# Expert lists in DRAM, token blocks as the stationary operand, routed rows added by DMA

## Chip, cores and metric

The kernel runs on one core of a Trainium2 chip. The metric is the time of one execution in device microseconds (us); the kernel before takes 2146.92 us, the median of three runs.

## What is computed

The reference is one step of a decoder layer for 1024 prompt tokens and 64 sample tokens, all in float32 with a model width of 1024. After a mixer stage comes the part that the change touches, a mixture of experts with 64 experts, 8 for each token, of hidden width 256:

```python
def swiglu(x, w_gate, w_up, w_down):
    return (jax.nn.silu(x @ w_gate) * (x @ w_up)) @ w_down
...
    scores = jax.nn.sigmoid(xf.astype(jnp.float32) @ w_router.astype(jnp.float32))
...
    _, idx = lax.top_k(jnp.where(emask, biased, -jnp.inf), TOP_K)
    sel = jnp.take_along_axis(scores, idx, axis=1)
    wts = (sel / jnp.sum(sel, axis=-1, keepdims=True) * ROUTED_SCALE).astype(xf.dtype)
    routed = routed_experts(xf, idx, wts, w_gate, w_up, w_down)
```

Each token's residual gets the weighted sum of its eight experts' outputs and a shared expert's. Then a per-layer embedding is added through a gate, `h + (p @ W_proj) * sigmoid(rmsnorm(h) @ W_gate)`, and a last norm gives the output.

## The kernel before

The names PE (TensorE), ACT (ScalarE), DVE (VectorE), POOL (GpSimd) and SP (SyncE) are those of the profile. Each stage is a block in which every engine runs its own instruction stream in order, and engines wait for each other by semaphores; a block ends when all engines are through. Tokens lie in 9 tiles of 128 (the last holds the 64 sample tokens).

**Router** (`router`, from L827). For each tile DVE normalises the rows (L1048), SP stores them to `rows_dram`, and PE computes the 64 scores and the shared expert. A long chain of small DVE operations picks the eight experts (`choose`), forms the weights (`weights`) and, from a running count, each token's place within its experts (`places`, L1124 to L1131). Places go to the table `place`, and the slot of every pair of token and expert to `slots`. At the end DVE works out `slots` and the number of rounds. A round handles up to CAP = 212 tokens of every expert; here there is one round.

**Experts** (`experts`, L1255 to L1566). Each expert's up to 212 tokens are two blocks, 128 and 84 rows (`BLK`). The matmuls have float32 accuracy out of reduced-precision ones: each operand x is split into hi(x), which ACT rounds, and lo(x) = x - hi(x), which DVE subtracts, and `three` (L1361) adds hi*hi, hi*lo and lo*hi. Weights are split the same way in each expert (L176, L183): 3 MB from DRAM into `raw_g`, `raw_u`, `raw_d`, one buffer each, by SP. For expert m:

- The list is made two experts ahead: DVE compares the places with 1 to 212 (`one_hot`, L1504), 18 small PE matmuls turn that into token numbers (`make_list`, L1374), DVE makes them integers (`to_index`, L1516), and POOL gathers the rows with two indirect DMAs (L1352).
- PE transposes the rows of the next expert (L1387), ACT and DVE split them (`x_hi`, `x_lo`).
- The gate and up products have the weights as the stationary operand and all 212 tokens as the moving one: 96 matmuls into two banks, transposed. After the sigmoid (L1479) DVE forms the hidden values and splits them.
- The down product has a block of tokens as the stationary operand and 512 columns of weights as the moving one: 12 matmuls for the first block, 12 for the second, which a branch on the expert's count skips (L1406 to L1412).
- ACT copies the result (L1457) and stores both blocks to `y_dram` (L1464).

The order on PE is gate and up, list, transposes of the next expert, down:

```python
                with pe.Fori(0, E) as n:
                    pe.wait_ge(x_lo_ev, 4 * (r * NJ + n) + 5)
                    gate_up(r * E + n)
                    make_list(r * NL + n + 2, r * NH + n + 2, 4 * (r * NJ + n) + 5)
                    transposes(r * NJ + n + 1, r * NL + n + 2)
                    down(r * E + n)
```

**Output** (`output`, L1573). For each tile POOL gathers the eight expert rows of each token from `y_dram` (`gathers`, L1652), and DVE adds them with their weights to the residual in SBUF (`gather_sum`, L1784). Then come the norm (L1789), the transposes (L1704), the gate matmuls (L1713), the projection (L1722), the injection and the last norm (L1812).

## Time and profile before

| | |
|---|---|
| time, median of 3 runs (lowest to highest) | 2146.92 us (2145.25 to 2151.26) |
| profiled execution, first to last instruction | 2147.0 us |
| PE busy | 1883.8 us (88%) |
| DVE busy | 1348.0 us (63%) |
| ACT busy | 868.2 us (40%) |
| POOL busy | 400.5 us (19%) |
| read from and written to DRAM | 330.71 and 66.34 MB |

The profiled execution's own time is its span: the page gives no other, and it equals the median to 0.1 us. A busy share is a mean over stages with different limits, so the stretches and timelines of the section on rows say more.
### The profile page before, as it was taken

What the parts mean: (1) busy time and instruction counts of PE and PEld (TensorE: products, weight loads), DVE (VectorE), ACT (ScalarE), POOL (GpSimd) and SP (SyncE); (2) the same over time, 40 slices, a digit from 0 to 9 for tenths busy, and PEclk for the clock granted to TensorE, in tenths of its full rate; (3) what the DMA queues carried; (4) which work ended last, traced back from release to release, by engine and by line L of the source; (5) the groups of instructions that cost most, each with busy time, mean ns of one, the idle gap of its engine ahead of it and who ended that gap; (6) DMA issues with size and microseconds to landing.
All of it is one profiled execution on the core that took longest, in us unless ns stands there. A gap on an engine that the chain in (4) does not pass through costs nothing. (4 is left out here: it accounts for less than half of the span.)

```text
span 2147.0 us, 35537 instructions
## 1 busy us (share of the span) xinstructions
PE 1883.8 (88%) x12638; PEld 1525.1 (71%) x12639; DVE 1348.0 (63%) x2002; ACT 868.2 (40%) x1392; POOL 400.5 (19%) x367
## 2 busy tenths in 40 slices
PE   7999999789968998899999989989989898747887
PEld 4566665457757897888888878888888798633433
DVE  3333433269856786767777777767666677556774
ACT  2122222133224555455555545555545555431111
POOL 0100001000011111211111121121111112135662
PEclk9999999889979998999999999999989899878999
DMA  9000000210066776767777777777676687655652
GB/s 358 35 0 0 0 0 13 85 52 29 30 208 221 255 267 219 258 225 252 263 251 246 258 244 248 251 258 264 227 254 235 226 277 247 214 203 179 229 199 103
DMA packets 104971, 396.27 MB, mean 185 GB/s; under 512 B 13230, under 2 KB 26990, under 8 KB 87901
## 3 DMA queue, kind: packets, MB, share of 16 engines
q1 hardware_dynamic: 61877, 245.27, 34.3%
q0 software_dynamic: 27264, 95.08, 13.0%
q10 hardware_dynamic: 15808, 55.65, 6.4%
q8 instruction: 12, 0.20, 0.0%
q14 instruction: 10, 0.08, 0.0%
HBM read 330.71 MB, written 66.34 MB: 185 GB/s over the span
## 5 line engine op out<-in xcount | busy, mean ns | idle before, releaser
L1352 POOL DMA_INDIRECT rows<-rows_dram,idx x132 | 228.2, 1728 | 1085.0 <-issue 1085.0
L1364 PE MATMUL GU<-x_hi,hi_g 128*128 128x212 f32 x1024 | 283.2, 277 | 0.0
L1364 PE MATMUL GU<-x_hi,hi_u 128*128 128x212 f32 x1024 | 282.7, 276 | 0.0
L1364 PE MATMUL GU<-x_lo,hi_g 128*128 128x212 f32 x1024 | 281.6, 275 | 0.0
L1364 PE MATMUL GU<-x_hi,lo_g 128*128 128x212 f32 x1024 | 281.2, 275 | 0.0
L1364 PE MATMUL GU<-x_lo,hi_u 128*128 128x212 f32 x1024 | 280.7, 274 | 0.0
L1364 PE MATMUL GU<-x_hi,lo_u 128*128 128x212 f32 x1024 | 280.3, 274 | 0.0
L1387 PE MATMUL T<-ident,rows 128*128 128x128 f32 (+1 forms) x1040 | 149.3, 314 | 137.9 <-DMA rows<-rows_dram,idx 137.9
L1522 DVE TENSOR_TENSOR x_lo<-T,x_hi 128x424 fp32r<-128x424 f32 x260 | 145.5, 595 | 144.8 <-ACT x_hi L1447 135.8
L1387 PEld LDWEIGHTS T<-ident,rows 128*128 128x128 f32 (+1 forms) x1040 | 132.9, 178 | 140.9 <-issue 140.9
L183 DVE TENSOR_TENSOR lo_u<-raw_u,hi_u 128x2048 fp32r<-128x2048 f32 x65 | 149.0, 2293 | 124.8 <-ACT hi_u L176 124.8
L1447 ACT ACTIVATE x_hi<-T 128x424 fp32r<-128x424 f32 x260 | 125.1, 527 | 220.1 <-PE T L1387 219.9
L1364 PEld LDWEIGHTS GU<-x_hi,hi_g 128*128 128x128 f32 x1024 | 197.3, 193 | 3.8
L1364 PEld LDWEIGHTS GU<-x_lo,hi_g 128*128 128x128 f32 x1024 | 197.3, 193 | 2.9
L1364 PEld LDWEIGHTS GU<-x_hi,lo_g 128*128 128x128 f32 x1024 | 197.6, 193 | 0.0
L1364 PEld LDWEIGHTS GU<-x_hi,hi_u 128*128 128x128 f32 x1024 | 196.6, 192 | 0.0
L1364 PEld LDWEIGHTS GU<-x_lo,hi_u 128*128 128x128 f32 x1024 | 196.6, 192 | 0.0
L1364 PEld LDWEIGHTS GU<-x_hi,lo_u 128*128 128x128 f32 x1024 | 196.6, 192 | 0.0
L1457 ACT ACTIVATE y<-Y 128x512 f32<-128x512 f32 (+1 forms) x256 | 150.8, 602 | 97.0 <-PE Y L1364 76.3
L183 DVE TENSOR_TENSOR lo_g<-raw_g,hi_g 128x2048 fp32r<-128x2048 f32 x65 | 148.8, 2290 | 60.5 <-ACT hi_g L176 60.5
L183 DVE TENSOR_TENSOR lo_d<-raw_d,hi_d 128x2048 fp32r<-128x2048 f32 x65 | 149.4, 2298 | 47.9 <-ACT hi_d L176 47.9
L1364 PE MATMUL Y<-hi_d,h_hi 128*128 128x512 f32 (+1 forms) x384 | 173.6, 452 | 0.0
(240 smaller groups left out, 3481.0 us busy)
## 6 DMA issues: line engine op xcount, KB each, us to landing
raw_g<-in_w_exp_gate SPq DMA_DIRECT2D x65, 1024.0 KB, 7.0
raw_u<-in_w_exp_up SPq DMA_DIRECT2D x65, 1024.0 KB
raw_d<-in_w_exp_down SPq DMA_DIRECT2D x65, 1024.0 KB, 7.7
y_dram<-y ACTq DMA_DIRECT2D x64, 512.0 KB
y_dram<-y ACTq DMA_DIRECT2D x64, 336.0 KB
rows_dram<-row SPq DMA_DIRECT2D x9, 512.0 KB, 2.7
w_big<-in_w_in SPq DMA_DIRECT2D x2, 2048.0 KB, 12.4
w_out<-in_w_out SPq DMA_DIRECT2D x1, 4096.0 KB, 18.1
```

The source lines that it names most:

```text
L183: dve.tensor_tensor(lo[:], raw[:], hi[:].bitcast(F32), ALU.subtract).then_inc(keep[f"lo_set_{name}"], 1)
L1352: pool.indirect_dma_start(out=rows[0:BLK[b], b, :], out_offset=None, in_=rows_dram[:, :], in_offset=bass.IndirectOffsetOnAxis(ap=idx[0:BLK ...
L1364: ins = pe.matmul(out, lhs[x], rhs[w], start=first and i == 0, stop=last and i == 2)
L1387: ins = pe.transpose(bank[:, k * CAP + b * P:k * CAP + b * P + BLK[b]], rows[0:BLK[b], b, (2 * i + k) * P:(2 * i + k + 1) * P], ident[0:BL ...
L1447: act.activation(x_hi[:, 2 * i:2 * i + 2, :], T[i][:, 0:2 * CAP].rearrange("p (k q) -> p k q", k=2), ACT.Copy).then_inc(x_hi_ev, 1)
L1457: act.activation(y[0:BLK[b], b, half * 512:(half + 1) * 512], Y[half][0:BLK[b], :], ACT.Copy).then_inc(y_ev, 1)
L1522: dve.tensor_tensor(x_lo[:, w, :], T[i][:, 0:2 * CAP].rearrange("p (k q) -> p k q", k=2), x_hi[:, w, :].bitcast(F32), ALU.subtract).then_i ...
```

## The change

**Router.** `place`, `slots` and the matmuls and comparisons on one-hot tables are gone. For each tile DVE works out, for each of the eight experts of a token, its position in a list in DRAM, and POOL scatters pairs (token number, weight) there with eight indirect DMAs. The list is filled beforehand, by a DMA in the mixer stage, with zero weights and spare rows (`list0`). At the stage's end SP loads the whole list as a table, and DVE copies it into `idx_t` (token numbers) and `w_t` (weights). SP also stores the residual with the shared expert's part to `acc_dram`, tile by tile.

**Experts.** The two blocks have buffers and semaphores of their own. A block of tokens is the stationary operand of the gate and up products, and 512 columns, 256 of the gate weights and 256 of the up weights, are the moving one: 24 matmuls a block, tokens on the partitions. The hidden values are then transposed (two PE transposes a block) before they are split. PE branches once for each expert: with 128 tokens or fewer the second block's matmuls and transposes are left out. ACT, DVE and POOL handle both blocks in any case. Gate and up splits have two buffers, and weights are loaded and split in halves. ACT scales the result with the weights `w_t` as it copies it, and POOL adds the rows to `acc_dram` with an indirect DMA that accumulates, one for each block; it waits until both of the expert before have landed. Gathers go out an expert ahead.

**Output.** The gathers and weighted sums are gone; SP loads the residual from `acc_dram`.

The diff, cut to its core: first the split helpers, then the router (DVE, SP, POOL, DVE), the experts (POOL, PE, ACT, DVE) and the output.

```diff
+def split_hi(act, keep, m, e, par, h):
+    act.wait_ge(keep[f"{m}_ld{h}"], 16 * e + 16)
+    act.activation(part_of(keep, "hi", m, par, h), part_of(keep, "raw", m, par, h),
+                   ACT.Copy).then_inc(keep[f"hi_set_{m}"], 1)
+def split_lo(dve, keep, m, e, par, h):
+    dve.wait_ge(keep[f"hi_set_{m}"], 2 * e + h + 1)
+    dve.tensor_tensor(part_of(keep, "lo", m, par, h), part_of(keep, "raw", m, par, h),
+                      part_of(keep, "hi", m, par, h).bitcast(F32), ALU.subtract).then_inc(keep[f"lo_set_{m}"], 1)
...
-                own.did(dve.tensor_copy(place[:, 0:E, t], pe_pos[:]))
+                own.did(dve.tensor_tensor(
+                    past[:], pos8[:].rearrange("p (k r) -> p k r", r=1).broadcast_to([P, TOP, ROUNDS - 1]),
+                    limits.rearrange("p (a r) -> p a r", a=1).broadcast_to([P, TOP, ROUNDS - 1]), ALU.is_gt))
+                own.wait()
+                own.did(dve.tensor_reduce(spot[:, 0, :], past[:], AX.X, ALU.add))
+                own.wait()
+                own.did(dve.scalar_tensor_tensor(out=spot[:, 1, :], in0=spot[:, 0, :], scalar=float(ROUND_ROWS - CAP),
+                                                 in1=pos8[:], op0=ALU.mult, op1=ALU.add))
+                own.wait()
+                own.did(dve.scalar_tensor_tensor(out=spot[:, 2, :], in0=spot[:, 1, :], scalar=float(E), in1=idx8[:],
+                                                 op0=ALU.mult, op1=ALU.add))
+                own.wait()
+                dve.tensor_scalar(lidx[:, t, :], spot[:, 2, :], -float(E), None, ALU.add).then_inc(listed, 1)
...
+                if t:
+                    sp.wait_ge(y_added, 2 * t)
+                    sp.dma_start(acc_dram[(t - 1) * P:t * P], resid[:, t - 1, :]).then_inc(acc_st, 16)
+            sp.wait_ge(y_added, 2 * TILES)
+            sp.dma_start(acc_dram[LAST * P:TOKENS], resid[:, LAST, :]).then_inc(acc_st, 16)
+            sp.wait_ge(list_st, 16 * TOP * TILES)
+            for b in range(2):
+                sp.dma_start(tab[:, b].rearrange("p (r e) a -> p r (e a)", e=E),
+                             list_dram.rearrange("(r b p e) a -> b p r (e a)", b=2, p=P, e=E)[b]).then_inc(tab_ld, 16)
+            sp.wait_ge(row_st, 16 * TILES)
+            sp.wait_ge(zero_st, 64)
...
+                pool_after(pool, keep["passed"], listed, t + 1)
+                for k in range(TOP):
+                    pool.indirect_dma_start(
+                        out=list_dram[:, :], out_offset=bass.IndirectOffsetOnAxis(ap=lidx[0:n, t, k:k + 1], axis=0),
+                        in_=lw[0:n, t, k, :], in_offset=None).then_inc(list_st, 16)
...
+            dve.wait_ge(tab_ld, 32)
+            for b in range(2):
+                own.did(dve.tensor_copy(keep["idx_t"][:, b, 0:PAIRS], tab[:, b, :, 0]))
+                own.did(dve.tensor_copy(keep["w_t"][:, b, :], tab[:, b, :, 1]))
...
-                with pool.Fori(0, NL) as k:
-                    pool_after(pool, keep["passed"], idx_ready, r * NL + k + 2)
-                    pool_after(pool, keep["passed"], x_tr, 4 * (r * NJ + k) + 1)
-                    for b in range(2):
-                        pool.indirect_dma_start(
-                            out=rows[0:BLK[b], b, :], out_offset=None, in_=rows_dram[:, :],
-                            in_offset=bass.IndirectOffsetOnAxis(ap=idx[0:BLK[b], b:b + 1], axis=0),
-                        ).then_inc(rows_ld, 16)
+            def gather(b, m):
+                n = BLK[b]
+                own.did(pool.tensor_copy(from_row[b][0:n, :], idx_t[0:n, b, bass.ds(m, 1)]))
+                own.wait()
+                pool.indirect_dma_start(
+                    out=rows[b][0:n, :], out_offset=None, in_=rows_dram[:, :],
+                    in_offset=bass.IndirectOffsetOnAxis(ap=from_row[b][0:n, 0:1], axis=0)).then_inc(rows_ld[b], 16)
+            def scatter(b):
+                n = BLK[b]
+                pool.indirect_dma_start(
+                    out=acc_dram[:, :], out_offset=bass.IndirectOffsetOnAxis(ap=to_row[0:n, b:b + 1], axis=0),
+                    in_=y[b][0:n, :], in_offset=None, compute_op=ALU.add).then_inc(y_st[b], 16)
+            def pair(m, par):
+                pool_after(pool, keep["passed"], rows_ld[1], 16 * m + 16)
+                pool_after(pool, keep["passed"], x_tr[1], 2 * m + 2)
+                gather(1, m + 1)
+                pool_after(pool, keep["passed"], x_tr[0], 2 * m + 4)
+                gather(0, m + 2)
+                for b in range(2):
+                    pool_after(pool, keep["passed"], y_st[b], 16 * m + 16)
+                own.did(pool.tensor_copy(to_row[:], idx_t[:, :, bass.ds(m, 1)].rearrange("p b a -> p (b a)")))
+                own.wait()
+                pool_after(pool, keep["passed"], y_ev[1], 2 * m + 2)
+                scatter(0)
+                pool_after(pool, keep["passed"], y_ev[1], 2 * m + 3)
+                scatter(1)
+                own.clear()
...
+                pool.dma_start(output_weights(keep)[1][:, b, :], a["w_ple_proj"][0, b * P:(b + 1) * P, :]).then_inc(
+                    y_st[b], 16)
+            gather(0, 0)
+            gather(1, 0)
...
-            def gate_up(m):
-                for mat, off in (("g", 0), ("u", CAP)):
-                    pe.wait_ge(lo_set[mat], m + 1)
-                    for f in range(FC):
-                        for k in range(KC):
-                            w = slice(f * P, (f + 1) * P)
-                            ins = three(GU[f][:, off:off + CAP], (hi[mat][:, k, w], lo[mat][:, k, w]),
-                                        (x_hi[:, k, :], x_lo[:, k, :]), k == 0, k == KC - 1)
-                        if mat == "u":
-                            ins.then_inc(gu_done, 1)
-                    if mat == "g":
-                        ins.then_inc(g_used, 1)
-                with pe.Fori(0, E) as n:
-                    pe.wait_ge(x_lo_ev, 4 * (r * NJ + n) + 5)
-                    gate_up(r * E + n)
-                    make_list(r * NL + n + 2, r * NH + n + 2, 4 * (r * NJ + n) + 5)
-                    transposes(r * NJ + n + 1, r * NL + n + 2)
-                    down(r * E + n)
+            def gate_up(b, m, par):
+                n = BLK[b]
+                pe.wait_ge(h_lo_ev[b], m + 1)
+                for k in range(KC):
+                    if k % 4 == 0:
+                        pe.wait_ge(x_lo_ev[b], 2 * m + k // 4 + 3)
+                        for mat in "gu":
+                            pe.wait_ge(lo_set[mat], 2 * m + k // 4 + 1)
+                    ins = three(GU[b][0:n, :].rearrange("p (m f) -> p m f", m=2), (x_hi[b][:, k, :], x_lo[b][:, k, :]),
+                                (hi_gu[par][:, :, k, :], lo_gu[par][:, :, k, :]), k == 0, k == KC - 1)
+                ins.then_inc(gu_done[b], 1)
+            def two_blocks(m, par):
+                gate_up(0, m, par)
+                transposes(1, m)
+                transposes(0, m + 1)
+                h_transposes(0, m)
+                gate_up(1, m, par)
+                down(0, m, 0, 1)
+                h_transposes(1, m)
+                down(0, m, 1, 1)
+                down(1, m, 0, 1)
+                down(1, m, 1, 1)
+            def one_block(m, par):
+                pe.sem_inc(x_tr[1], 2)
+                pe.sem_inc(gu_done[1], 1)
+                pe.sem_inc(h_tr[1], 1)
+                gate_up(0, m, par)
+                transposes(0, m + 1)
+                h_transposes(0, m)
+                down(0, m, 0, 2)
+                down(0, m, 1, 2)
+            def pair(m, par):
+                filled = pe.value_load(keep["fill"][0:1, bass.ds(m, 1)], min_val=0, max_val=SEQ + NS)
+                with pe.If(filled > P):
+                    two_blocks(m, par)
+                with pe.If(filled < P + 1):
+                    one_block(m, par)
+            pe.wait_ge(blank, 3)
+            transposes(0, 0)
+            each_pair(pe, pair)
...
+            def weighted(b, m, half):
+                act.wait_ge(y_done[half], 2 * m + b + 1)
+                if half == 0:
+                    act.wait_ge(y_st[b], 16 * m + 16)
+                act.sem_inc(act_passed, 1)
+                act.activation(y[b][0:BLK[b], half * 512:(half + 1) * 512], Y[half][0:BLK[b], :], ACT.Copy,
+                               scale=w_t[0:BLK[b], b, bass.ds(m, 1)]).then_inc(y_ev[half], 1)
+            def pair(m, par):
+                for h in range(2):
+                    split_hi(act, keep, "d", m, 0, h)
+                for name in "gu":
+                    for h in range(2):
+                        split_hi(act, keep, name, m + 1, 1 - par, h)
+                sigmoid(0, m)
+                x_high(1, m)
+                x_high(0, m + 1)
+                h_high(0, m)
+                sigmoid(1, m)
+                weighted(0, m, 0)
+                h_high(1, m)
+                weighted(0, m, 1)
+                weighted(1, m, 0)
+                weighted(1, m, 1)
...
-                    split_lo(dve, keep, "g", m + 1)
-                    hidden(m, 0)
-                    hidden(m, 1)
-                    x_parts(r * NJ + n + 1)
-                    split_lo(dve, keep, "u", m + 1)
-                    to_index(r * NL + n + 2)
-                    one_hot(r * NL + n + 3, following)
-                    split_lo(dve, keep, "d", m + 1)
+            def pair(m, par):
+                for h in range(2):
+                    split_lo(dve, keep, "d", m, 0, h)
+                for h in range(2):
+                    split_lo(dve, keep, "g", m + 1, 1 - par, h)
+                split_lo(dve, keep, "u", m + 1, 1 - par, 0)
+                hidden(0, m)
+                x_low(1, m)
+                x_low(0, m + 1)
+                h_low(0, m)
+                split_lo(dve, keep, "u", m + 1, 1 - par, 1)
+                hidden(1, m)
+                h_low(1, m)
+                own.clear()
...
-                        for k in range(TOP):
-                            pool.indirect_dma_start(
-                                out=yk[:, k, :], out_offset=None, in_=table,
-                                in_offset=bass.IndirectOffsetOnAxis(ap=idx[:, k:k + 1], axis=0)).then_inc(y_ld[k], 16)
-            def gather_sum(t, ks):
-                    dve.scalar_tensor_tensor(out=resid[:, t, :], in0=yk[:, k, :], scalar=wk[:, k:k + 1],
-                                             in1=resid[:, t, :], op0=ALU.mult, op1=ALU.add).then_inc(added, 1)
+            rows = acc_dram[0:TOKENS].rearrange("(t p) d -> p t d", p=P)
+            sp.dma_start(resid[:, 0, :], rows[:, 0, :]).then_inc(h0_ld, 16)
+            sp.dma_start(g_ple[:], a["g_ple"][0:1, :].broadcast_to([P, D])).then_inc(out_st, 16)
+            sp.dma_start(resid[:, 1:TILES, :], rows[:, 1:TILES, :]).then_inc(h_ld, 16)
```

What the engines execute changes most at three places of the expert loop. On PE, a stretch before, from the last gate/up matmul over the list to the transposes of the next expert (`T` is a PSUM bank, `tok` the token numbers, and `ISA` and `REGISTER_ALU` rows hold waits and address arithmetic):

```order
L1364 MATMUL GU<-x_hi,lo_u 128x212
L1369 ISA
L1370 ISA
L1374 MATMUL T<-tok,hot_slots 128x2 x18
L1380 ISA
L1384 ISA
L1387 MATMUL T<-ident,rows 128x128
L1387 MATMUL T<-ident,rows 128x84
```

The same stretch in the change, for an expert with one block (`hid` are the hidden values):

```order
L1356 MATMUL GU<-hi_gu,x_lo 128x512
L1362 ISA
L1364 ISA
L1366 MATMUL T<-ident,rows 128x128 x4
L1364 REGISTER_ALU
L1366 MATMUL T<-ident,rows 128x128 x4
L1385 REGISTER_ALU
L1387 MATMUL GU<-ident,hid 128x128 x2
L1356 MATMUL Y<-hi_d,h_hi 128x512
```

The list is gone, the transposes are one block's, and the hidden values' transposes stand between them and the down part. On ACT, the middle of an expert before, where the weight splits lie among the result's copies:

```order
L176 ACTIVATE hi_u<-raw_u 128x1024
L1483 ISA
L1456 REGISTER_ALU
L1457 ACTIVATE y<-Y 128x512
L176 ACTIVATE hi_u<-raw_u 128x1024
L1456 REGISTER_ALU
L1457 ACTIVATE y<-Y 128x512
```

And the start of an expert in the change:

```order
L185 ACTIVATE hi_d<-raw_d 128x1024
L185 ACTIVATE hi_d<-raw_d 128x1024
L184 ISA
L185 ACTIVATE hi_gu<-raw_g 128x1024
L185 ACTIVATE hi_gu<-raw_g 128x1024
L185 ACTIVATE hi_gu<-raw_u 128x1024
L185 ACTIVATE hi_gu<-raw_u 128x1024
L1451 ACTIVATE sig<-GU 128x256
```

All six half-splits now stand ahead of the sigmoid. On POOL, an expert before:

```order
L1348 ISA
L75 ISA
L1352 DMA rows<-rows_dram,idx 128x1024
L1352 DMA rows<-rows_dram,idx 84x1024
L1348 REGISTER_ALU
```

And in the change:

```order
L1306 COPY from_row<-idx_t 84x1
L1308 DMA rows<-rows_dram,from_row 84x1024
L77 REGISTER_ALU
L1306 ISA
L1306 COPY from_row<-idx_t 128x1
L1308 DMA rows<-rows_dram,from_row 128x1024
L1328 ISA
L1328 COPY to_row<-idx_t 128x2
L1314 DMA acc_dram<-y,to_row 1408x1024
L77 REGISTER_ALU
L1314 DMA acc_dram<-y,to_row 1408x1024
```

The gathers come first, each after a copy of its index, and the two scatters stand behind them.

## Rows read from the trace of the kernel before

**Rows 1.** Stretches: length, busy us (count) of PE, PEld, DVE, ACT, POOL; clock, DMA.
```profile
440.00:597.00 157.00, 135.08 (x899) 109.45 (x897) 132.22 (x415) 52.10 (x75) 9.57 (x26) 0.96 0.10 38
...
614.00:1902.00 1288.00, 1158.74 (x9490) 1082.74 (x9490) 898.53 (x1151) 676.96 (x956) 221.21 (x128) 0.93 0.72 245
1902.00:1941.00 39.00, 2.77 (x11) 1.86 (x10) 19.96 (x16) 5.85 (x9) 19.21 (x22) 0.55 0.54 182
1941.00:2147.00 206.00, 174.73 (x440) 80.17 (x440) 138.08 (x126) 36.91 (x68) 110.82 (x118) 0.94 0.52 184
```

**Rows 2.** Timeline of PE in one expert: start, us, engine, line, operation, count.
```profile
627.44 0.28 PE L1364 MATMUL GU<-x_lo,hi_u 128*128 128x212 f32 x1
627.55 0.27 PE L1364 MATMUL GU<-x_hi,lo_u 128*128 128x212 f32 x1
...
628.14 1.70 PE L1387 MATMUL T<-ident,rows 128*128 128x128 f32 x16
...
630.40 0.40 PE L1364 MATMUL Y<-hi_d,h_hi 128*128 128x512 f32 x1
630.63 0.39 PE L1364 MATMUL Y<-lo_d,h_hi 128*128 128x512 f32 x1
```

**Rows 3.** Groups by line and shape, PE: busy us, mean ns, idle before.
```profile
L1364 PE MATMUL Y<-hi_d,h_hi 128*84 128x512 f32 x128 | 50.2, 392 | 0.0
```

**Rows 4.** Waits between 614 and 1902 us: total, times, longest.
```profile
PE T L1387 <- DMA rows<-rows_dram,idx: 129.1, 34, 7.3
```

**Rows 5.** Stretches around one stall of PE (columns as in Rows 1).
```profile
687.00:691.00 4.00, 0.00 (x0) 0.00 (x0) 1.36 (x4) 0.00 (x0) 0.00 (x0) 0.99 1.02 282
691.00:694.40 3.40, 3.20 (x17) 3.20 (x18) 1.43 (x3) 1.65 (x4) 0.00 (x0) 0.50 0.61 249
694.40:698.00 3.60, 3.60 (x17) 2.73 (x17) 1.54 (x3) 3.43 (x5) 0.00 (x0) 1.00 0.00 0
```

**Rows 6.** Groups by line and shape, ACT (columns as in Rows 3).
```profile
L176 ACT ACTIVATE hi_u<-raw_u 128x1024 fp32r<-128x1024 f32 x130 | 138.8, 1068 | 0.0
...
L1457 ACT ACTIVATE y<-Y 128x512 f32<-128x512 f32 x128 | 78.2, 611 | 28.7 <-PE Y L1364 28.4
...
L1014 ACT ACTIVATE sg<-RG 128x256 f32<-128x256 f32 x9 | 3.5, 384 | 20.7 <-PE RG L966 20.7
```

**Rows 7.** Groups by line and shape, DVE (columns as in Rows 3).
```profile
L183 DVE TENSOR_TENSOR lo_u<-raw_u,hi_u 128x2048 fp32r<-128x2048 f32 x65 | 149.0, 2293 | 124.8 <-ACT hi_u L176 124.8
...
L1522 DVE TENSOR_TENSOR x_lo<-T,x_hi 128x424 fp32r<-128x424 f32 x260 | 145.5, 595 | 144.8 <-ACT x_hi L1447 135.8
...
L1139 DVE TENSOR_TENSOR hid<-sg,RU 128x256 f32<-128x256 f32 x9 | 3.8, 421 | 0.8
...
L1124 DVE SCALAR_TENSOR_TENSOR pe_pos<-RC,maskf 128x64 f32<-128x64 f32 x9 | 2.0, 217 | 0.0
```

**Rows 8.** Groups by line and shape, POOL (columns as in Rows 3).
```profile
L1352 POOL DMA_INDIRECT rows<-rows_dram,idx x132 | 228.2, 1728 | 1085.0 <-issue 1085.0
L1652 POOL DMA_INDIRECT yk<-y_dram,idx_k x72 | 86.7, 1204 | 26.2 <-issue 26.2
```

**Rows 9.** DMA issues: tiles, queue, operation, count, median us from issue to landing.
```profile
rows<-rows_dram,idx POOLq DMA_INDIRECT x132, 6.6
```

**Rows 10.** Timeline between the router and the first expert.
```profile
591.02 1.28 DVE L1150 TENSOR_TENSOR resid<-RY,resid 128x512 f32<-128x512 f32 x2
...
609.86 3.08 PE L1387 MATMUL T<-ident,rows 128*128 128x128 f32 x16 [8.88 <-DMA rows<-rows_dram,idx]
```

**Rows 11.** Timeline of the output stage: its start, and its last tile.
```profile
1914.39 0.33 SPq L1626 DMA_DIRECT2D g_ple<-in_g_ple  x1
...
1941.53 16.72 PE L1713 MATMUL OG<-w_big,colT 128*128 128x512 f32 x32 [0.88 <-DVE colT L1796]
...
2119.76 13.90 PE L1713 MATMUL OG<-w_big,colT 128*128 128x512 f32 x32
...
2133.50 3.60 PE L1722 MATMUL OJ<-w_big,pT 128*128 128x512 f32 x8
```

More of the change, by code:

```diff
@@ L140, in build @@
-        with ExitStack() as split:
-            for m in "gud":
-                for part in ("hi", "lo"):
-                    name = f"{part}_{m}"
-                    keep[name] = split.enter_context(nc.sbuf_tensor(name, keep[f"raw_{m}"].shape, F32R))
-                    keep[f"{part}_set_{m}"] = ctx.enter_context(nc.semaphore(f"{part}_set_{m}"))
-            router(nc, a, c, keep, rows_dram, y_dram)
-            experts(nc, a, c, keep, rows_dram, y_dram)
-        output(nc, a, o, keep, y_dram)
+            **{n: sem(n) for n in ("router_ld", "output_ld", "passed")},
@@ L1405, in down, with transposes @@
-            def down(m):
+            def transposes(b, m):
+                n = BLK[b]
+                pe.wait_ge(rows_ld[b], 16 * m + 16)
+                for i in range(2):
+                    pe.wait_ge(x_lo_ev[b], 2 * m + i + 1)
+                    for k in range(4):
+                        ins = pe.transpose(T[b][i][:, k * n:(k + 1) * n], rows[b][0:n, (4 * i + k) * P:(4 * i + k + 1) * P],
+                                           ident[0:n, 0:n])
+                    ins.then_inc(x_tr[b], 1)
@@ L1497, in _ @@
+            for half in range(2):
+                act.sem_inc(y_ev[half], 1)
+            act.wait_ge(blank, 3)
+            x_high(0, 0)
+            each_pair(act, pair)
         @block.vector
```

649 lines of the change are left out of this document (247 added, 402 removed).

## Prediction

> **What bounds the kernel now.** I read the stretches first: the program is a row of stages, and a change is worth what it does in its own stage [rows 1]. Four matter. The router (440 to 597 us) is DVE's: 132.2 of 157 us busy. The expert loop (614 to 1902) takes 1288 us for 64 experts, 20.1 us each, with TensorE at a mean granted clock of 0.93. Then 39 us pass until the output stage's first large matmul, and its nine tiles take 206 us.
>
> Inside the loop I read the timeline of PE [rows 2]: matmuls of 212 columns follow each other every 0.11 us, those of 512 columns every 0.23 us. An expert has 96 of the first (10.6 us), the list matmuls (0.6), 16 transposes (1.7 with its drain) and 12 or 24 of the second (2.8 or 5.5): 15.5 us with one token block in the down part, 18.3 with two. The 84-row form of the down matmul occurs 128 times, 4 to an expert, so 32 experts have two blocks and 32 one [rows 3]. Dense, that is 32 x 15.5 + 32 x 18.3 = 1082 us. The other 206 us are stalls: PE waits 129 us in 34 waits for gathered rows [rows 4], because the gather is issued only when the list is made, late in the expert before. What each stall does to the clock stands in [rows 5]: 0.99 while PE idles from 687 to 691, then 0.50 until 694.4, then 1.00 again. The stall is paid twice.
>
> **The change, part by part.** The sum is made against the profiled span of 2147.0 us, which is also the median of the three runs (2146.92); a difference under 0.3% (6 us) couldn't be told from none.
>
> *Router: +7 us.* Per tile five small DVE operations make the list index (about 0.22 us each, the price of the small operation in [rows 7]) and two small copies go: +1.0 us, nine times, on the engine that bounds the stage. The low half of expert 0's down weights (2.3 us, [rows 7]) moves to the expert loop. Bounds: 0 and +11. POOL gets eight scatters a tile; at the 1.2 us of the output stage's indirect DMAs [rows 8] that is 10 us of a 16 us tile, so DVE's next normalisation isn't held up.
>
> *Handover: +15 us.* Before, 18.8 us lie between the start of DVE's last residual add (591.0) and the first expert transposes (609.9) [rows 10]. Now the last tile's eight scatters (11 us with the wake-up), their landing (3), the table load (5), four casts (2), the block change (1), two weight DMAs on POOL ahead of the first gather (2), that gather's issue (2) and its landing come in a row: the last is 6.6 us in [rows 9], more here because the weights of expert 1 and two other loads start beside it, so 8. Together 34: +15. Bounds: +5, if the landings overlap, and +30.
>
> *Expert loop: -66 us.* PE's own work hardly changes with two blocks: 24 matmuls of 512 columns per block are 5.5 us, twice 11.0 against 10.6. With one block it falls from 15.5 to 9.3 us (5.5 + 0.8 transposes + 0.2 + 2.8). The lists in DRAM let the gathers go out an expert ahead, so the wait of [rows 4] goes. What is late next is ACT. Its cycle starts with six half-splits at 1.07 us less 0.07 of overlap (6.0 us, [rows 6]), then the sigmoid (0.4); DVE, a half-split behind, makes the hidden rows (2 x 0.42, [rows 7]) by 7.7 us. One block: DVE's four low parts of the next rows (2.4 us, from 0.6 for 424 elements) and the low part of the hidden rows (0.4) end at 10.5; PE's down part takes 2.8; ACT has three weighted copies left (0.6 each less overlap, [rows 6]): 14.8 us with the semaphore steps. Two blocks: the second gate/up starts at 8.5, ends at 14.1, the down part and two transposes take 5.7, the last copy 0.6: 20.4 us. At full clock 32 x 14.8 + 32 x 20.4 = 1126 us, 162 less than now.
>
> But with one block PE works 9.3 of 14.8 us, and its two stalls (1 us before the hidden transposes, 2.7 before the down part) lie together with 0.2 us of work between. Stalls of this size are what [rows 5] shows ahead of a fall. I take a fall in three experts of four, 48 in all. Half clock for 3.4 us costs PE at most 1.7 us, for two such stretches (gate/up restarts slowly) 3.4, and not all of it on the cycle: 2 us each, 96 us. So 1222 us, against 1288. Bounds: none falls, 1126; each expert loses 3.4 us, 1344.
>
> The matmul price decides much of this. The row says 0.23 us for 512 columns of a stream that loads new weights each time [rows 2]. The Trainium skill ("TensorE: Matmul & The Clock Gate", Back-to-back issue gap) gives about 131 ns as the sustained figure at 512 columns. By that figure 48 matmuls of the two-block cycle would give back 4.8 us, and 12 of the one-block cycle 1.2: some 190 us less. The trace contradicts the page here. By the row the loop is 1222 us, and I go by the row.
>
> *The accumulating scatter: 0.* No row shows a DMA that adds. The nearest is the plain gather of the same rows, 6.6 us to landing [rows 9]; POOL's issue, 1.7 us on average [rows 8], makes four indirect DMAs and their wake-ups about 11 us, under the cycle. The scatter must read its target as well, so from 6.6 us up to three times that. ACT's first weighted copy of the next expert waits for it; between the scatter's issue and that copy lie some 10 us with one block and 15 with two. I take 8 us, nearer the gather's row: hidden. At 20 us it would cost 10 x 32 + 5 x 32 = 480.
>
> *Weights.* They are loaded in halves; each raw buffer has a cycle less 3 to 6 us to be refilled. The loop moves 245 GB/s at a DMA share of 0.72 [rows 1], so 340 at full share. Now 3.2 MB of weights, 0.9 gathered and 0.9 scattered are 5.0 MB, 5.8 if the read counts: 14.6 to 17 us of DMA against a mean cycle of 19.1. Hidden, with little room.
>
> *Output: -46 us.* The 72 gathers and the 72 weighted sums go; the residual is read back, 0.5 MB first. From SP's first DMA to the first large matmul 27.1 us pass now [rows 11]; without the gathers it is the load (4), the norm (6) and the transposes (2): 12, so -15. Tiles follow every 22.3 us (from 1941.5 to 2119.8 in eight steps, [rows 11]). PE needs 13.7 for the gate matmuls (the step from 2119.76 to 2133.50), 3.6 for the others and 1 for transposes: 18.4, so -31. The other engines have less per tile. Bounds: -30 and -55.
>
> Sum: 2147 + 7 + 15 - 66 - 46 = 2057 us.
>
> **Rivals.** *The clock holds.* The stalls are shorter than the 4 us of [rows 5], and PE then needs no recovery: 2057 - 96 = 1961 us. For it: each stall alone is under 3 us. Against: they lie close together.
>
> *The scatter chain sets the cycle: slower.* The next scatter waits for both earlier ones to land, and ACT waits for the same. With a landing of 16 us the one-block cycle grows by 6 and the two-block cycle by 1: 32 x 7 = 224, so 2281 us. It decides the sign from about 12.8 us on (2.8 x 32 = 90 us, the whole gain). For it: adding needs a read of the target that no row prices, on engines already 0.72 busy. Against: gathers of the same rows take half of that. The Trainium skill ("DMA: Bandwidth & Descriptors", SDMA does more than copy) describes the add as a reduction of two streams inside the DMA engine; no run so far shows its speed.
>
> *DMA bound.* At 17 us of DMA an expert, the one-block cycle can't fall below 17: with the clock's share it stood at about 16.3, so 32 x 0.8 = 26 us more, 2083.
>
> *Matmuls overlap better.* If in the new order the loads of new weights hid so well that 512 columns took half of 0.23 us, 48 matmuls of the two-block cycle would give 5.5 us and 12 of the one-block cycle 1.4: 221 us less, 1836. Against: [rows 2], the same form at 0.23. The Trainium skill's figure above would make this the likely case.
>
> *It does little*: the second block's branch is seldom skipped. Then 64 x 20.4 = 1306 for the loop, 2141. [Rows 3] speak against it.
>
> **How the numbers follow.** The forecast has 0.53, the clock that holds 0.18, the scatter chain 0.15, the DMA bound 0.11, the better overlap 0.01, the little effect 0.02. Slower is the chain, 0.15; the little effect counts as the same, 0.02; the rest is faster, 0.83. The range reaches down to the clock that holds (1961) and up to a landing of about 13.5 us (3.5 x 32 = 112 more, 2170), 1960 to 2170; what is left out is a chain slower than that, and a clock that holds while the handover or the output gains more than I took.
>
> **What would show it.** Right: in the loop no wait of PE for gathered rows; ACT's splits start each cycle and ACT is busy almost throughout its first half; two cycle lengths, near 15 to 17 and 20 to 22 us; a clock near 0.9; output tiles every 18.4 us with PE above 0.95 busy. Wrong: ACT's weighted copies waiting for the scatter, scatters landing after more than 10 us; splits waiting for weight loads; the first gate/up more than 25 us later than before.

## The result and the profile after

The changed kernel takes 2046.79 us (median of four runs, 2046.58 to 2050.64), the kernel before beside it 2146.09 us (2143.22 to 2151.26): a ratio of 0.954, 95% interval 0.951 to 0.958. The forecast was 2057 us, in 1960 to 2170. The profiled execution went from 2147.0 to 2044.8 us, 102.2 less where the sum had 90. By its terms:

| term | forecast | measured | read from |
|---|---|---|---|
| router | +7 | +9.0 | start of DVE's last residual add: 591.02, now 600.01 |
| handover, to the first transposes | +15 | +11.8 | 18.84 us from there, now 30.62 |
| from there to the first gate/up | not listed | -2.1 | 4.83 us, now 2.75: only one block is transposed first |
| expert loop | -66 | -71.9 | 1287.4 us, now 1215.5 (first gate/up to the last down matmul) |
| output: start | -15 | -17.3 | 39.4 us, now 22.1 |
| output: tiles and end | -31 | -31.7 | 205.5 us, now 173.8; from the second tile on one every 18.26 us |

The rows behind the table, first the two of the kernel before that [rows 10] and [rows 11] don't show (start, us, engine, line, operation):

```profile
614.69 0.53 PE L1364 MATMUL GU<-x_hi,hi_g 128*128 128x212 f32 x1
...
1901.72 0.40 PE L1364 MATMUL Y<-hi_d,h_lo 128*128 128x512 f32 x1
```

and those of the changed kernel:

```profile
600.01 1.28 DVE L1175 TENSOR_TENSOR resid<-RY,resid 128x512 f32<-128x512 f32 x2
...
616.07 0.36 DVE L1211 CAST idx_t<-tab 128x384 int32<-128x384 f32 x1 [13.35 <-DMA tab<-list_dram]
...
630.63 1.94 PE L1366 MATMUL T<-ident,rows 128*128 128x128 f32 x8 [31.42 <-DMA rows<-rows_dram,from_row]
633.38 0.77 PE L1356 MATMUL GU<-hi_gu,x_hi 128*128 128x512 f32 x1 [0.81 <-DVE x_lo L1501]
...
1848.48 0.40 PE L1356 MATMUL Y<-hi_d,h_lo 128*128 128x512 f32 x1
...
1870.96 15.87 PE L1668 MATMUL OG<-w_big,colT 128*128 128x512 f32 x32 [0.88 <-DVE colT L1741]
```

The stretches of the changed kernel, with the columns of [rows 1]: length, busy us of PE, PEld, DVE, ACT and POOL with counts, then granted clock, DMA share and GB/s.

```profile
440.00:600.00 160.00, 140.72 (x904) 111.51 (x902) 134.66 (x428) 50.38 (x75) 78.92 (x86) 0.94 0.21 77
601.00:630.00 29.00, 0.00 (x0) 0.00 (x0) 4.20 (x16) 0.00 (x0) 10.65 (x14) 0.51 0.54 182
633.00:1849.00 1216.00, 1021.74 (x4416) 751.53 (x4416) 713.34 (x1026) 712.28 (x1150) 464.76 (x447) 0.91 0.89 259
1849.00:1871.00 22.00, 2.70 (x11) 1.93 (x11) 2.67 (x2) 3.85 (x7) 5.05 (x8) 0.54 0.67 205
1871.00:2045.00 174.00, 165.37 (x440) 77.04 (x440) 56.68 (x61) 37.26 (x68) 14.99 (x41) 0.97 0.10 38
```

In the last row PE works 165 of 174 us: the output stage is PE's alone, and what it gained is what POOL's gathers and DVE's sums had held back. In the loop the clock is lower than before (0.91, it was 0.93) and DMA busier (0.89, it was 0.72), yet the loop is shorter. The waits in the loop (us in total, times, longest) say what PE waits for now:

```profile
PE GU L1387 <- DVE hid L1509: 117.8, 63, 3.1
...
PE Y L1356 <- DVE h_lo L1514: 58.7, 32, 1.9
...
PE T L1366 <- DMA rows<-rows_dram,from_row: 31.4, 1, 31.4
```

The 34 waits for gathered rows of [rows 4] are gone but for the very first. In their place PE waits for the hidden values, once in nearly every expert, and again before the down part in the 32 experts with one block: 176 us, more than the 129 us of waits that went. The loop is shorter all the same, because a one-block expert has much less for PE to do. No row has ACT waiting for a scatter. A cycle is the time from ACT's first half-split of an expert to that of the next. ACT's timeline shows them (start, us, engine, line, operation):

```profile
656.12 2.00 ACT L185 ACTIVATE hi_d<-raw_d 128x1024 fp32r<-128x1024 f32 x2
...
672.63 2.00 ACT L185 ACTIVATE hi_d<-raw_d 128x1024 fp32r<-128x1024 f32 x2
674.53 2.00 ACT L185 ACTIVATE hi_gu<-raw_g 128x1024 fp32r<-128x1024 f32 x2
676.43 1.99 ACT L185 ACTIVATE hi_gu<-raw_u 128x1024 fp32r<-128x1024 f32 x2
678.32 0.36 ACT L1451 ACTIVATE sig<-GU 128x256 f32<-128x256 f32 x1
...
689.54 2.00 ACT L185 ACTIVATE hi_d<-raw_d 128x1024 fp32r<-128x1024 f32 x2
...
711.44 1.05 ACT L185 ACTIVATE hi_d<-raw_d 128x1024 fp32r<-128x1024 f32 x1
```

Experts 1 and 2 have one block (16.5 and 16.9 us), expert 3 has two (21.9). The sigmoid of expert 2 comes at 678.32, behind six half-splits; PE had that expert's gate/up through at 676.2:

```profile
676.16 1.04 PE L1366 MATMUL T<-ident,rows 128*128 128x128 f32 x8
680.33 0.69 PE L1387 MATMUL GU<-ident,hid 128*128 128x128 f32 x2 [3.13 <-DVE hid L1509]
682.69 0.80 PE L1356 MATMUL Y<-hi_d,h_hi 128*128 128x512 f32 x1 [1.67 <-DVE h_lo L1514]
683.28 0.63 PE L1356 MATMUL Y<-lo_d,h_hi 128*128 128x512 f32 x1
683.71 0.63 PE L1356 MATMUL Y<-hi_d,h_lo 128*128 128x512 f32 x1
```

The two stalls lie together as the prediction had them, with other sizes: 3.13 and 1.67 us where it took 1 and 2.7. The down matmuls behind them follow every 0.43 us, not every 0.23. The stretches of that moment have the clock:

```profile
676.20:680.30 4.10, 1.00 (x9) 0.76 (x7) 4.07 (x6) 4.10 (x8) 3.51 (x5) 0.98 0.94 233
680.30:683.70 3.40, 1.70 (x4) 1.12 (x5) 3.40 (x7) 0.68 (x3) 0.51 (x1) 0.50 1.05 320
683.70:687.00 3.30, 3.30 (x9) 2.62 (x8) 1.06 (x4) 0.89 (x2) 0.19 (x1) 0.51 1.03 295
687.00:690.40 3.40, 3.40 (x16) 2.76 (x16) 0.09 (x1) 2.59 (x4) 1.08 (x1) 1.00 0.99 401
```

0.50 is the lower of the two levels, 1.2 GHz. Here the clock had fallen when the first stall ended (0.98 up to 680.30, 0.50 from there), before the second began. Expert 1, whose expert before has two blocks, has a short stall first, and the fall comes behind the second one (its down matmuls, too, follow every 0.43 us):

```profile
663.80 0.44 PE L1387 MATMUL GU<-ident,hid 128*128 128x128 f32 x2 [0.91 <-DVE hid L1509]
666.16 0.55 PE L1356 MATMUL Y<-hi_d,h_hi 128*128 128x512 f32 x1 [1.92 <-DVE h_lo L1514]
666.51 0.63 PE L1356 MATMUL Y<-lo_d,h_hi 128*128 128x512 f32 x1
666.94 0.63 PE L1356 MATMUL Y<-hi_d,h_lo 128*128 128x512 f32 x1
```

```profile
665.00:668.50 3.50, 2.34 (x6) 1.90 (x7) 2.99 (x6) 0.00 (x0) 0.06 (x1) 0.71 1.04 307
```

Each of the 31 whole one-block cycles has such a stretch, and of the 32 two-block cycles 14 of the 16 that follow a one-block expert, after a single stall of about 2.5 us, and the very first; the two kinds take 16.77 and 21.27 us on average, 20.58 a two-block cycle at full clock.

### The profile page after: what moved, and what is told of

The parts are those of the page before. It is cut to its first block and busy times, and to the rows that moved or that the text cites. A ratio compares the mean times of both kernels' runs of the same rounds, so it can differ in the third digit from the quotient of the medians.

```text
span 2044.8 us, 25818 instructions
## 1 busy us (share of the span) xinstructions
PE 1741.0 (85%) x7538; PEld 1191.5 (58%) x7539; DVE 1065.5 (52%) x1822; ACT 898.9 (44%) x1581; POOL 611.2 (30%) x668
## 5 line engine op out<-in xcount | busy, mean ns | idle before, releaser
L1314 POOL DMA_INDIRECT acc_dram<-y,to_row x128 | 217.4, 1698 | 526.4 <-ACT y L1466 455.3
L1356 PE MATMUL GU<-hi_gu,x_hi 128*128 128x512 f32 (+1 forms) x768 | 315.8, 411 | 18.1 <-issue 16.7
L1356 PE MATMUL GU<-lo_gu,x_hi 128*128 128x512 f32 (+1 forms) x768 | 312.4, 407 | 0.0
L1356 PE MATMUL GU<-hi_gu,x_lo 128*128 128x512 f32 (+1 forms) x768 | 312.3, 407 | 0.0
L1466 ACT ACTIVATE y<-Y,w_t 128x512 f32<-128x512 f32 (+1 forms) x256 | 168.6, 684 | 276.4 <-PE Y L1356 276.4
L192 DVE TENSOR_TENSOR lo_d<-raw_d,hi_d 128x1024 fp32r<-128x1024 f32 x128 | 151.2, 1222 | 264.1 <-ACT hi_d L185 264.1
L1308 POOL DMA_INDIRECT rows<-rows_dram,from_row x131 | 162.3, 1239 | 42.5 <-POOL from_row L1306 37.7
L1356 PE MATMUL Y<-lo_d,h_hi 128*128 128x512 f32 (+1 forms) x384 | 173.5, 452 | 0.0
L1356 PE MATMUL Y<-hi_d,h_lo 128*128 128x512 f32 (+1 forms) x384 | 172.2, 449 | 0.0
L435 PE MATMUL S<-w_big,colT 128*128 128x512 f32 (+3 forms) x432 | 160.9, 530 | 1.7 <-DMA w_big<-in_w_in 1.7
L192 DVE TENSOR_TENSOR lo_gu<-raw_u,hi_gu 128x1024 fp32r<-128x1024 f32 x130 | 157.9, 1215 | 0.0
```

The source lines that it names most:

```text
L192: dve.tensor_tensor(part_of(keep, "lo", m, par, h), part_of(keep, "raw", m, par, h), part_of(keep, "hi", m, par, h).bitcast(F32), ALU.subt ...
L435: ins = pe.matmul(bank[0:n, 0:n1 - n0], colT[:, k, 0:n], w_in[:, k, n0:n1], start=(k == 0), stop=(k == KC - 1))
L1308: pool.indirect_dma_start(out=rows[b][0:n, :], out_offset=None, in_=rows_dram[:, :], in_offset=bass.IndirectOffsetOnAxis(ap=from_row[b][0: ...
L1314: pool.indirect_dma_start(out=acc_dram[:, :], out_offset=bass.IndirectOffsetOnAxis(ap=to_row[0:n, b:b + 1], axis=0), in_=y[b][0:n, :], in_ ...
L1356: ins = pe.matmul(out, lhs[x], rhs[w], start=first and i == 0, stop=last and i == 2)
L1466: act.activation(y[b][0:BLK[b], half * 512:(half + 1) * 512], Y[half][0:BLK[b], :], ACT.Copy, scale=w_t[0:BLK[b], b, bass.ds(m, 1)]).then_ ...
```

## The experiments

The theory after this reading: a one-block cycle is the chain of splits, sigmoid, hidden values and down part that the prediction added up to 14.8 us, plus a clock fall; scatter and weights are hidden (nothing waits for them). The rivals: DMA holds the one-block cycle (0.89 of 1216 us is 16.9 us an expert, close to the 16.77 seen), or the scatter that adds does. Cycles are read as above, as means of 31 and 32; clock and DMA share are those of the loop.

| run | median us | ratio to before (95%) | one block | two blocks | clock | DMA |
|---|---|---|---|---|---|---|
| the change | 2046.79 | 0.954 (0.951 to 0.958) | 16.77 | 21.27 | 0.91 | 0.89 |
| filled stalls | 2000.11 | 0.935 (0.932 to 0.937) | 15.44 | 21.19 | 0.97 | 0.91 |
| scatter without add | 2044.72 | 0.956 (0.953 to 0.959) | 16.77 | 21.28 | 0.91 | 0.77 |
| always two blocks | 2147.21 | 1.002 (1.000 to 1.004) | - | 20.60 | 1.00 | 0.84 |
| early sigmoid | 1961.85 | 0.916 (0.913 to 0.919) | 15.91 | 19.59 | 0.94 | 0.95 |
| both | 1929.23 | 0.899 (0.897 to 0.902) | 14.42 | 19.90 | 0.99 | 0.97 |
| the three together | 1917.36 | 0.894 (0.892 to 0.896) | 14.28 | 19.60 | 1.00 | 0.92 |
| 4 rows for 84, alone | 2046.85 | 0.955 (0.952 to 0.958) | 16.69 | 21.27 | 0.91 | 0.83 |
| three, other handover | 1906.70 | 0.889 (0.887 to 0.891) | 14.39 | 19.56 | 1.00 | 0.92 |

**Filled stalls.** In the branch with one block PE gets matmuls that nobody uses (ACT's sigmoid of the second block, whose result nobody uses either, now waits for the first four):

```diff
-                pe.sem_inc(gu_done[1], 1)
                 pe.sem_inc(h_tr[1], 1)
                 gate_up(0, m, par)
+                pe.wait_ge(h_lo_ev[1], m + 1)
+                for k in range(4):
+                    ins = pe.matmul(GU[1][0:BLK[1], :]..., x_hi[0][:, k, 0:BLK[1]], hi_gu[par][:, :, k, :], ...)
+                ins.then_inc(gu_done[1], 1)
                 transposes(0, m + 1)
                 h_transposes(0, m)
+                pe.wait_ge(lo_set["d"], 2 * m + 2)
+                pe.wait_ge(y_ev[0], 2 * m + 1)
+                for k in range(7):
+                    pe.matmul(Y[0][0:BLK[1], :], h_hi[1][:, k % 2, :], hi_d[:, k % 2, 0:512], ...)
                 down(0, m, 0, 2)
```

> In the one-block branch TensorE gets 4 matmuls of 512 columns after gate/up and 7 before the down part, whose results nobody uses; they fill its two stalls. Theory (the clock fall is what the one-block cycle has over 14.8 us): the down part runs at 0.23 us a matmul instead of 0.43, the one-block cycle goes from 16.8 to about 15.1 us, the two-block cycles behind one lose their 1.4 us: 32 x 1.7 + 15 x 1.4 = 75 us less, about 1970, clock near 0.99 in the loop. Rival (the weights or the scatter set the one-block cycle): the clock rises, but ACT's splits then wait for the up weights, whose landing has little slack now: less than 25 us gained, 2020 or more. Rival (the stalls are not what the clock answers to): clock unchanged, time the same or up to 30 us longer.

2000 us, 47 less; the theory had 75. The loop, and the end of a filled stall, with the down matmuls 0.23 us apart:

```profile
633.00:1805.00 1172.00, 1049.81 (x4767) 763.86 (x4765) 712.92 (x1024) 716.20 (x1152) 465.68 (x447) 0.97 0.91 268
```

```profile
1209.56 1.88 PE L1428 MATMUL Y<-hi_d,h_hi 128*84 128x512 f32 x7
...
1212.06 0.39 PE L1356 MATMUL Y<-lo_d,h_hi 128*128 128x512 f32 x1
1212.29 0.39 PE L1356 MATMUL Y<-hi_d,h_lo 128*128 128x512 f32 x1
```

Of the 31 one-block cycles 21 now run without a half-clock stretch, and they take 15.0 us: the chain's 14.8, found by filling the stalls. The clock's price is so 1.8 us for a one-block cycle (16.77 less 15.0) and 1.5 for a two-block one. What is missing is in the other 10, where 2.2 us or more of the first stall were left behind a one-block expert, and in 12 two-block cycles behind such an expert, whose stall of 2.5 us wasn't filled: they still fall. The same 2.2 us were left in 5 more cycles and the clock held; why it fell in some and not in others stays open. In one place the first rival shows as well, in the fourth of four one-block experts in a row. ACT's timeline there:

```profile
1219.44 1.07 ACT L185 ACTIVATE hi_gu<-raw_g 128x1024 fp32r<-128x1024 f32 x1
1221.17 1.06 ACT L185 ACTIVATE hi_gu<-raw_g 128x1024 fp32r<-128x1024 f32 x1 [0.66 <-DMA raw_g<-in_w_exp_gate]
1222.40 1.06 ACT L185 ACTIVATE hi_gu<-raw_u 128x1024 fp32r<-128x1024 f32 x1 [0.18 <-DMA raw_u<-in_w_exp_up]
1225.80 1.06 ACT L185 ACTIVATE hi_gu<-raw_u 128x1024 fp32r<-128x1024 f32 x1 [2.34 <-DMA raw_u<-in_w_exp_up]
```

The splits wait for weights, in a stretch (columns as above) where DMA is busy throughout:

```profile
1220.00:1230.00 10.00, 4.27 (x20) 2.83 (x19) 7.16 (x11) 6.26 (x11) 5.20 (x6) 0.77 1.04 313
```

**Scatter without add.**

```diff
-                    in_=y[b][0:n, :], in_offset=None, compute_op=ALU.add).then_inc(y_st[b], 16)
+                    in_=y[b][0:n, :], in_offset=None).then_inc(y_st[b], 16)
```

> The scatters overwrite the rows in DRAM instead of adding to them (the sum over a token's experts is left out). Theory (the add is hidden): same time within 0.3% (2041 to 2053), scatters landing in 5 to 6.5 us instead of 6.5. Rival (adding reads its target on engines that are busy at a share of 0.89, so weights and gathers land later): without the add the loads land 1 us or more sooner and the loop gets over 10 us shorter, below 2037.

2044.7 us against 2046.8, and the intervals of the ratio overlap (0.953 to 0.959 and 0.951 to 0.958): no cost of the add shows. DMA issues of the changed kernel (count, KB, median us from issue to landing):

```profile
rows<-rows_dram,from_row POOLq DMA_INDIRECT x131, 8.9
acc_dram<-y,to_row POOLq DMA_INDIRECT x128, 6.5
```

and without the add, in the loop:

```profile
raw_g<-in_w_exp_gate SPq DMA_DIRECT2D x126, 512.0 KB, 7.2
...
acc_dram<-y,to_row POOLq DMA_INDIRECT x126, 3.8
```

with the loop's stretch:

```profile
633.00:1845.00 1212.00, 1017.85 (x4407) 748.59 (x4406) 712.17 (x1023) 711.19 (x1147) 371.79 (x447) 0.91 0.77 259
```

Without the add the scatters land sooner than the theory's 5 to 6.5 us. So adding takes 2.7 us more to land, and 0.12 of the DMA time of the loop (2.3 us an expert). The gate weights land in 7.2 us, 9.5 with the add; nobody was waiting for them.

**Always two blocks.**

```diff
-                with pe.If(filled > P):
+                with pe.If(filled > -1):
...
-                with pe.If(filled < P + 1):
+                with pe.If(filled < 0):
```

> TensorE takes the branch with two blocks for every expert. Theory: all 64 cycles are the two-block cycle of 20.6 us and none has a stall long enough for the clock to fall: 64 x 20.6 = 1318 for the loop instead of 1216, about 2149, as long as the kernel before, with no half-clock stretch in the loop. Rival (the second block's matmuls are cheap, since PE waits for ACT anyway): under 40 us more, below 2087.

2147.2 us where 2149 stood, and a loop at full clock:

```profile
633.00:1945.00 1312.00, 1226.67 (x5868) 882.34 (x5867) 714.22 (x1023) 719.30 (x1147) 425.80 (x446) 1.00 0.84 240
```

This is as long as the kernel before (ratio 1.002). What the output stage gains (49 us) the longer loop, router and handover take back, so the net gain of the change, 100 us, is as large as what the 32 experts save that skip the second block. No run takes the gathers an expert ahead, the lists in DRAM or the tokens as the stationary operand by itself, so what each of them is worth stays open.

**Early sigmoid.** ACT (and DVE likewise) does the up weights behind the hidden values:

```diff
-                for name in "gu":
-                    for h in range(2):
-                        split_hi(act, keep, name, m + 1, 1 - par, h)
+                for h in range(2):
+                    split_hi(act, keep, "g", m + 1, 1 - par, h)
                 sigmoid(0, m)
                 x_high(1, m)
                 x_high(0, m + 1)
                 h_high(0, m)
+                for h in range(2):
+                    split_hi(act, keep, "u", m + 1, 1 - par, h)
```

> ACT makes the sigmoid and the copies behind it before the two half-splits of the up weights, DVE likewise. Theory (ACT's six half-splits ahead of the sigmoid set both cycles): hidden rows come up to 1.9 us sooner; 1 to 1.9 us off every cycle, 64 to 120 us less, 1925 to 1985. Rival (the up weights become late): the split and the low part of the up weights move 4 us later, gate/up of the next expert waits for them and their loads start later: same or slower, 2040 to 2100.

1961.9 us, within the theory:

```profile
633.00:1765.00 1132.00, 992.60 (x4415) 734.64 (x4413) 714.18 (x1023) 714.32 (x1148) 448.73 (x447) 0.94 0.95 278
```

The two-block cycle at full clock falls from 20.58 to 19.50 us, and none but the very first has a half-clock stretch: behind a one-block expert the stall ahead of the hidden transposes shrank from 2.5 us to between 1.1 and 1.4. One-block cycles are 0.9 us shorter, still with the fall in 28 of 31.

**Both, and fewer rows.** Then both edits in one kernel; and, on top of them or alone, 4 rows instead of 84 in the second gather and scatter of an expert with one block:

```diff
+            def by_fill(e, move, b):
+                filled = pool.value_load(keep["fill"][0:1, bass.ds(e, 1)], ...)
+                with pool.If(filled > P):
+                    move(b, BLK[b])
+                with pool.If(filled < P + 1):
+                    move(b, 4)
...
-                scatter(1)
+                by_fill(m, scatter, 1)
```

> The early sigmoid and the filled stalls together. Theory (by the trace of the early sigmoid, the DMA engines are the ceiling: 0.89 of 1216 us in the changed kernel is 16.9 us of DMA per expert, whatever its number of blocks): a single one-block expert runs its 14.4 us, in a run of them the splits wait for weights and it is 16 us or more; 1935 to 1962, no more than 27 us under the early sigmoid alone. Rival (chain and clock add up freely): 32 x (16.0 - 14.4) = 50 us less, about 1910.

> As the two together, and where an expert has one block, its second gather and its second scatter move 4 rows (of padding) instead of 84. Theory (DMA is the ceiling there): a one-block expert has 80 of 212 rows less to gather and to add, about 2.5 us of its 16.9 us of DMA; one-block cycles of about 14.4 us also in a run: 1895 to 1920. Rival (DMA is not what the two together wait for): within 6 us of the two together.

> The changed kernel with nothing but the 4 rows instead of 84. Theory (there the DMA work is hidden behind chain and clock): 2041 to 2053, the same; fewer DMA records, share about 0.82. Rival (it is DMA bound already, and the one-block cycle of 16.8 us is the DMA's 16.9): 32 x 1.5 = 48 us less, under 2010.

Alone the fewer rows change nothing (2046.85 us; DMA share 0.83 for 0.89):

```profile
633.00:1845.00 1212.00, 1017.19 (x4414) 747.54 (x4413) 712.78 (x1024) 711.04 (x1150) 453.72 (x446) 0.91 0.83 242
```

In the changed kernel the DMA work is hidden, and 16.9 us of it beside a cycle of 16.8 was a coincidence. Both edits give 1929.2 us, below the theory's 1935: it took 16.9 us as a floor, but second and third one-block experts in a row mostly ran in 13.9 us. Waits of a microsecond and more for weights remain in the third cycle of one run of four (16.0 us), in the fourth of the other (15.9) and in a few two-block cycles behind a one-block expert. With the fewer rows those two cycles take 13.87 us too, and the kernel 1917.4, 12 less than with both edits: this is where DMA held it. The stretches, first with both edits, then with the three:

```profile
633.00:1729.00 1096.00, 1025.09 (x4768) 750.07 (x4766) 718.25 (x1023) 720.18 (x1150) 466.28 (x447) 0.99 0.97 287
```

```profile
633.00:1716.00 1083.00, 1018.05 (x4768) 745.23 (x4768) 717.50 (x1025) 718.33 (x1150) 460.73 (x447) 1.00 0.92 271
```

**The handover.** The changed kernel's first gather lands in 10.6 us, beside loads of 4 MB. First these loads were held back:

```diff
             ple = keep["ple"]
+            sp.wait_ge(rows_ld[0], 16)
```

with the output weights' load moved behind the first gathers on POOL.

> The first gathers go out before the two loads of the output weights on POOL, and SP holds the loads of the token extras and of the second expert's weights until the first gather has landed. Theory (the first gather takes 10.7 us because these loads share the engines): it lands in about 7 us, the first gate/up starts 4 to 6 us sooner. Rival (a first gather is slow by itself): it lands in 10 us again, and only the 1.2 us of issue are gained.

The gather lands in 4.4 us and the first gate/up starts at 625.2 instead of 633.4 us, more than the theory had. The time is 2046.4 us in a single run, the same. ACT's timeline of that run shows the loan paid back in the first expert, whose cycle takes 29.8 us instead of 22.3:

```profile
625.66 2.00 ACT L185 ACTIVATE hi_d<-raw_d 128x1024 fp32r<-128x1024 f32 x2 [0.60 <-issue]
634.24 1.06 ACT L185 ACTIVATE hi_gu<-raw_g 128x1024 fp32r<-128x1024 f32 x1 [6.58 <-DMA raw_g<-in_w_exp_gate]
```

So the second expert's gate and up weights were loaded in the router instead, where the DMA share is 0.21, and each later load of them one place earlier; this and the edit above were put into the kernel with the three edits, which ran again beside it.

```diff
+            for name in "gu":
+                for h in range(2):
+                    sp.wait_ge(keep[f"lo_set_{name}"], h + 1)
+                    sp.dma_start(part_of(keep, "raw", name, 0, h), expert_weights(a, name, 1, h)).then_inc(...)
             sp.wait_ge(y_added, 2 * TILES)
...
-                    load(e, r * E + n)
+                    load("d", e, r * E + n)
+                    e = sp.snap(n + 2)
+                    load("gu", e, r * E + n + 1)
```

> The three together, and the handover mended: the router loads the gate and up weights of the second expert while the DMA engines have little to do, the token extras and the output weights are loaded behind the first gather. Theory (after the run in which holding these loads back gained 8 us and lost them in the first expert's cycle): the first gather lands in 4 to 6 us, the first gate/up starts at 625 to 628 us instead of 633 and the first cycle doesn't grow: 5 to 9 us less than the three together. Rival (the extra load of 2 MB at the end of the loop, which nobody uses, and the token extras push the output's first load back by as much): within 3 us of the three together.

> The three together once more, beside the run with the mended handover on one chip: the same as before, 1912 to 1921.

1906.7 us (ratio 0.889, 0.887 to 0.891) against 1914.3 (0.8935, 0.892 to 0.895): 7.6 us less, the theory. In the profiled executions it is 4.4: the first gate/up starts at 625.3 instead of 633.6 and the first cycle doesn't grow (21.2 us), but the second does (18.3 for 14.9), and the output's first large matmul comes 0.8 us later behind the loop. This is the fastest version of the study, 7% below the changed kernel.

## Why the prediction was right

**The expert loop.** 1222 us forecast, 1216 measured, with the chain right and the clock's part right partly by luck. The one-block cycle at full clock, 14.8 by the sum, is 15.0 (filled stalls); the two-block one, 20.4, is 20.6 (always two blocks). "What is late next is ACT" holds: moving two half-splits behind the sigmoid takes 85 us off. A fall "in three experts of four, 48 in all" had no row behind its count: 46 of 63 whole cycles have a stretch at half clock, but these are all one-block cycles and most two-block cycles behind one, not three of any four, so that the count came out by luck. The stalls were mis-sized as well: "1 us" and "2.7" are 0.7 to 1.3 and 1.9 us behind a two-block expert, and 2.7 to 3.1 and 1.7 to 1.9 behind a one-block one. The prediction's own 9.3 of 14.8 us leave 5.5 of idle PE, more than the 3.7 that it placed. "2 us each" was too much: 1.8 and 1.5. By these prices the 1216 us divide into 32 x 14.97 + 32 x 20.58 = 1138 and 31 x 1.80 + 15 x 1.47 = 78 (14.97 is the mean of the filled cycles at full clock without the one that waited for weights). The sum had 1126 and 96, two errors of opposite sign.

The reading of the loop before has a slip that the forecast doesn't use: its four terms of a dense expert (10.6, 0.6, 1.7 and 2.8 or 5.5) add up to 15.7 and 18.4 us, not 15.5 and 18.3, so that the stalls cost 197 us and not 206.

**The matmul price** in [rows 2] carried over to the new order: 0.23 us from one 512-column matmul with new weights to the next at full clock, 0.43 at half. The Trainium skill's 131 ns ("TensorE: Matmul & The Clock Gate", Back-to-back issue gap) would have taken some 190 us off the forecast, an estimate from that figure that gives about 1867 us. The trace disagrees with it in this stream, and the measurement decides. The rival of the better overlap (1836 us, at half of 0.23) fell with the same rows.

**The accumulating scatter: 0** was right with its size: 8 us to landing taken, 6.5 measured, between the bounds, and without the add 3.8. The Trainium skill ("DMA: Bandwidth & Descriptors", SDMA does more than copy) calls the add a reduction inside the engine; here it cost 2.7 us of landing and no time of the kernel that shows. The rival of the scatter chain fell with it: it needed 12.8 us.

**Weights: "hidden, with little room"** is what the runs show: removing DMA work gains nothing in the changed kernel (2044.7 and 2046.9 us) and 12 us once the cycles are 14 us. The DMA-bound rival was wrong here, and as a floor for each expert it stayed wrong: beside both edits single one-block cycles ran in 13.9 us. It came true only in part, in a few cycles behind one-block experts, once these were that short.

**The clock that holds (1961)** didn't: its 0.18 rested on each stall being under 3 us. Behind a one-block expert the first stall is about 3.1 us, and in 11 of 15 such cycles the clock had fallen by its end. But stalls of 0.7 to 1.3 and 1.9 us, with 0.4 us of work between, were followed by a fall in 16 of 16 cycles, and a single one of about 2.5 us in 14 of 16, so being under 3 us wasn't enough.

**Router and output** came within 2.4 us of each term. The one mis-sized term of note is in the **handover**: +15 forecast, +11.8 measured. No row was named for the scatters' landing (3) and the table load (5); from DVE's last add to the table's landing 16.1 us pass, where the pieces (11, 3 and 5) made 19. The gather was counted twice in part: [rows 9] has the time from the start of the issue, so that its 8 us held the issue's 2 already. It took 10.6 us, and the two errors nearly cancel (10 in the sum).

**It does little** fell with [rows 3], but its price was right: with the second block in every expert the sum gave 2141, and the run (always two blocks) 2147.

## What to carry to other kernels

When a wait goes, add up the chain that comes next, with its stalls: here PE waits longer in the new chain than it did in the old one, and the gain is as large as the work that half of the cycles no longer have. A stall needn't be long to be followed by a clock fall: here one of 2.5 us was in 14 of 16 cycles, and two of about 1 and 1.9 us close together in 16 of 16. So either move what PE waits for ahead of work that nobody waits for yet (85 us here), or put unused matmuls into the stall (47 us). Before holding a transfer back to speed up another, ask who waits for the one that is held: here the 8 us gained came back as a first cycle 7.5 us longer, and only moving it to a stage with idle DMA engines kept the gain.

## What the runs showed of the hardware that wasn't expected

- The first gather of 128 rows lands in 4.4 us with the loads held back, and in 10.6 beside 4 MB of them; in the loop the median of all gathers, of 128 and of 84 rows, is 8.9. The median of the kernel before (6.6) is none of these.
- A scatter that adds lands in 6.5 us, one that overwrites in 3.8, at a DMA share of 0.89 and 0.77.
- 11 matmuls without use in each one-block expert made the kernel 47 us faster: in 21 of 31 cycles the down matmuls behind them follow each other every 0.23 us instead of every 0.43.
- A stall of 2.5 us was followed by half clock in 14 of 16 cycles of the changed kernel; where the early sigmoid left 1.1 to 1.4 us of it, in none of 16.
